# Eight sample rows in column groups, small tiles for the widest recurrence levels, and two reordered casts in a two-layer decoder step

## What is computed

```python
x = x + 0.5 * gate0 * swiglu_1(mod(rmsnorm(x)))
h = mod(rmsnorm(x))
(u_pool, hq, hf, hi, hg, aq, ak, av, iq, ik, iw, gl) = split(h @ w_in)
ya = pool_mix(u_pool) 
yb = rmsnorm(hgrn_scan(hq, f(hf), 1 - f(hf), hi)) * silu(hg)
yc = sparse_attention(aq, ak, av, iq, ik, iw)
x = x + gate1 * (sum(sigmoid(gl_b) * (y_b @ w_b)) @ w_out)
x = x + 0.5 * gate2 * swiglu_2(mod(rmsnorm(x)))
```

## Time and profile before

| | us |
|---|---|
| median of three runs | 2718.54 |
| the three runs | 2718.4, 2721.93, 2718.54 |
| the profiled execution, its own time | 2719.41 |
| its span in the trace | 2717.3 |

### The profile page before, as it was taken

The page is one execution under the profiler, slowest core; times in us unless marked ns, Lnnn a source line. Parts: engine busy times, 40 slices in busy tenths (PEclk is TensorE's granted clock), DMA queues, the critical chain, the costliest instruction groups (busy, mean ns, idle before and its releaser), DMA issues. The chain is left out here.

```text
span 2717.3 us, 53697 instructions
## 1 busy us (share of the span) xinstructions
PE 2652.4 (98%) x22268; PEld 2517.3 (93%) x22268; DVE 922.8 (34%) x2323; ACT 831.4 (31%) x1313; POOL 1103.5 (41%) x886
## 2 busy tenths in 40 slices
PE   6999999999999999999999999999999999999998
PEld 4999998999888989999989999989998889899998
DVE  4111113266794441111131111134677824311111
ACT  2321222222465233212233212232234632332221
POOL 4434345333223354344553444542333225444443
PEclk9999999999999999999999999999999999999999
DMA  6334345312223343332533322641122134222222
GB/s 246 139 125 148 136 162 178 115 47 83 76 71 97 125 144 136 124 107 92 185 128 138 121 97 93 201 154 63 63 77 83 57 106 173 73 91 85 94 90 80
DMA packets 107055, 312.88 MB, mean 115 GB/s; under 512 B 18476, under 2 KB 45130, under 8 KB 89434
## 3 DMA queue, kind: packets, MB, share of 16 engines
q1 hardware_dynamic: 97952, 290.60, 31.8%
q10 hardware_dynamic: 8906, 19.44, 2.0%
HBM read 299.56 MB, written 10.66 MB: 114 GB/s over the span
## 5 line engine op out<-in xcount | busy, mean ns | idle before, releaser
L948 POOL TENSOR_TENSOR w_lo<-raw,w_hi 128x512 fp32r<-128x512 f32 (+1 forms) x800 | 1011.3, 1295 | 1579.2 <-ACT w_hi L1022 1531.6
L2163 PE MATMUL bank<-h_hi,w_hi 128*128 128x260 f32 x3744 | 1067.7, 285 | 2.9 <-ACT silu_g L1069 2.4
L2164 PE MATMUL bank<-h_hi,w_lo 128*128 128x260 f32 x3744 | 1053.9, 281 | 0.0
L2165 PE MATMUL bank<-h_lo,w_hi 128*128 128x260 f32 x3744 | 1053.7, 281 | 0.0
L2163 PEld LDWEIGHTS bank<-h_hi,w_hi 128*128 128x128 f32 x3744 | 703.6, 188 | 38.0 <-issue 35.9
L2164 PEld LDWEIGHTS bank<-h_hi,w_lo 128*128 128x128 f32 x3744 | 703.9, 188 | 0.0
L2165 PEld LDWEIGHTS bank<-h_lo,w_hi 128*128 128x128 f32 x3744 | 703.6, 188 | 0.0
L1022 ACT CAST w_hi<-raw 128x2048 fp32r<-128x2048 f32 (+3 forms) x219 | 376.4, 1719 | 481.1 <-PE bank L2165 376.9
L2163 PE MATMUL bank<-mid_hi,w_hi 128*128 128x260 f32 x1232 | 351.1, 285 | 0.0
L2165 PE MATMUL bank<-mid_lo,w_hi 128*128 128x260 f32 x1232 | 348.5, 283 | 0.0
L2164 PE MATMUL bank<-mid_hi,w_lo 128*128 128x260 f32 x1232 | 348.3, 283 | 0.0
(11 more groups left out here) (334 smaller groups left out, 3315.7 us busy)
## 6 DMA issues: line engine op xcount, KB each, us to landing
raw<-in_w SPq DMA_DIRECT2D x120, 1024.0 KB, 4.9
raw<-in_w SPq DMA_DIRECT2D x64, 512.0 KB, 4.4
raw<-in_w SPq DMA_DIRECT2D x32, 768.0 KB, 4.3
ada_ring<-in_ada SPq DMA_DIRECT2D x82, 256.0 KB, 5.3
raw<-in_w SPq DMA_DIRECT2D x32, 640.0 KB, 4.1
ada_ring<-in_ada SPq DMA_DIRECT2D x57, 320.0 KB, 5.3
ada_ring<-in_ada SPq DMA_DIRECT2D x57, 192.0 KB, 5.3
ada_low<-in_ada SPq DMA_DIRECT2D x20, 256.0 KB, 5.2
```

The source lines that it names most:

```text
L948: last = pool.tensor_tensor(w_lo[j][:, cols], raw[j][:, cols], w_hi[j][:, cols].bitcast(F32), ALU.subtract)
L2163: mm(out, wh(wb), xh(xb), start=(n == 0), stop=False)
L2164: mm(out, wl(wb), xh(xb), start=False, stop=False)
L2165: last = mm(out, wh(wb), xl(xb), start=False, stop=(n == len(blocks) - 1))
```

## The change

1. The padded sample group is gone. `sample_rows` multiplies the eight columns of `h_s` (stationary, 128 x 8) by the raw fp32 weights, in four matmuls of 64 weight columns per `k`, each into its own 32 rows of a PSUM bank (column tiles, as in the conditioning products). `sample_group` is all eight `k` of a name. u's and hi's rows run inside the `k` loop of `first_token`, aq0's ahead of its group 0, iq's, aq1's and kv's between kbT and delta, hg's at the last level of head 3. ACT copies the four pieces out, and clears three tiles a layer, whose padding was written with the group before.
2. Since TensorE now reads `raw`, SP's load of a slot also waits for the sample rows of the slot that lay there.
3. Level 32 is eight matmuls of 32 x 32, level 64 four of 64 x 64.
4. The filler moves up by one group, and head 0 has nothing between levels 32 and 64.
5. ACT copies kbT ahead of the cast.
6. POOL's held split no longer waits.

```diff
@@ SP @@
             def load_mix(l, slot):
                 j = slot % 2
                 sp.wait_ge(w_split[j], slot_use(l, "mix", slot // 2) + PRIMED)
+                if slot >= 2 and MIX[slot - 2] in TOKENS:
+                    wait_main(sp, mix_unit(l, MIX[slot - 2], 0))
...
             def load_gates(l, stage, slot, tiles):
+                if (stage, slot) == ("ga0", 1):
+                    wait_main(sp, mix_unit(l, "hg", 0))
@@ POOL @@
                         first = 0
-                        gap = N_SUB * l + {"up00": 0, "mix": 1, "up10": 2}.get(stage, 0)
-                        if gap > 0 and stage in ("up00", "mix", "up10"):
-                            split(l, stage, 0, 0)
-
-                            pool.wait_ge(h_lo_ready, 9 * gap + 2)
-                            split(l, stage, 0, 1)
-                            first = 1
                         with pool.Fori(first, slots // 2) as r:
@@ ACT @@
+                if u == 0:
+                    for a in range(4):
+                        src = bank[unit % 4][32 * a:32 * a + NB, 0:HD]
...
+                    last.then_inc(done, 1)
+                    return
...
-                if hf == 1:
-                    head_after(l, "mix", MIX.index(f"H{hd}"))
+                if hf == 1 and hd == 0:
+                    head_after(l, "mix", MIX.index("H0"))
...
+                zeros = h_hi[:, :, COLS:].bitcast(F32)
+                steps.note(s.copy(rot[:, TT].rearrange("p r n -> p (r n)").rearrange("p (k n) -> p k n", k=KT), zeros))
+                steps.note(s.copy(vals[:, TT].rearrange("p (k n) -> p k n", k=2), zeros[:, 0:2, 0:HD]))
+                steps.note(s.copy(h_g[:, TT].rearrange("p (k n) -> p k n", k=4), zeros[:, 0:4, 0:HD]))
...
                     turned_keys(l, hd)
+                    if hd + 1 < HH:
+                        head_after(l, "mix", MIX.index(f"H{hd + 1}"))
@@ PE @@
+            def sample_rows(l, name, k):
+                slot = MIX.index(name)
+                unit = mix_unit(l, name, 0)
+                if k == 0:
+                    pe.wait_ge(w_loaded[slot % 2], slot_loads(l, "mix", slot // 2))
+                    take_unit(unit)
+                for a in range(4):
+                    at = k * 256 + a * HD
+                    last = mm(bank[unit % 4][32 * a:32 * a + NB, 0:HD], h_s[:, k, :], raw[slot % 2][:, at:at + HD],
+                              start=(k == 0), stop=(k == KT - 1))
...
                 for k in range(KT):
                     wait_h(N_SUB * l + 1, k)
-                    for u in range(3 if k < KT - 1 else 2):
-                        token_tile(l, "u", u, 0, k)
...
+                    sample_rows(l, "u", k)
+                    for g in (0, 2):
+                        last = token_tile(l, "u", g, k)
+                    if k < KT - 1:
+                        sample_rows(l, "hi", k)
+                for g in (1, 3):
+                    for k in range(KT):
+                        last = token_tile(l, "u", g, k)
                     last.then_inc(main_full, 1)
+                sample_rows(l, "hi", KT - 1)
...
-                        if 1 <= n < 5 and hd + n > 1:
-                            token_group(l, BESIDE[hd], n)
-                        elif n >= 5 and hd + 1 < HH:
+                        if hd == 0 and n in (2, 3):
+                            token_group(l, BESIDE[0], n)
+                        elif hd == 0 and n in (4, 5, 6):
+                            hgrn_projection(l, 1, n - 4)
+                        elif hd > 0 and 1 <= n < 5:
+                            token_group(l, BESIDE[hd], n - 1)
+                        elif 0 < hd < HH - 1 and n >= 5:
                             hgrn_projection(l, hd + 1, n - 5)
...
+                            sample_group(l, "hg")
                             token_group(l, "hg", 0)
...
-                            last = mm(out[:, cs], hk[hd % 2][:, cs], qt[:, cs], start=True, stop=True)
+                            if n < MASKED:
+                                last = mm(out[:, cs], hk[hd % 2][:, cs], qt[:, cs], start=True, stop=True)
+                                continue
+                            for s0 in range(0, P, 2 * h):
+                                keys = slice(c * P + s0, c * P + s0 + h)
+                                rows = slice(c * P + s0 + h, c * P + s0 + 2 * h)
+                                last = mm(out[s0:s0 + h, rows], hk[hd % 2][:, keys], qt[:, rows], start=True, stop=True)
...
                     if hd + 1 < HH:
-                        token_group(l, BESIDE[hd + 1], 0)
+                        sample_group(l, BESIDE[hd + 1])
...
                 token_group(l, "hg", 3)
-                token_group(l, "hg", 4)
                 outputs(HH - 1)
```

More of the change, by code:

```diff
@@ L116 @@
 BESIDE = ("aq0", "iq", "aq1", "kv")
+TOKENS = ("u", "hi", "aq0", "iq", "aq1", "kv", "hg")
 MIX_SOURCE = {n: SLOT0["token"] + i for i, n in enumerate(("u", "hi", "hg", "aq0", "aq1", "kv", "iq", "thin"))}
@@ L1137, in token_unit @@
                 wait_main(act, unit)
-                tl = slice(2 * u, 2 * u + 2) if u < 2 else slice(TT, TT + 1)
-                nt = 2 if u < 2 else 1
-                src = bank[unit % 4][:, 0:256 * nt].rearrange("p (t n) -> p t n", t=nt)
                 done = main_taken[unit % 4]
+                if u == 0:
+                    for a in range(4):
+                        src = bank[unit % 4][32 * a:32 * a + NB, 0:HD]
+                        cols = slice(a * HD, (a + 1) * HD)
+                        if name == "u":
+                            last = s.copy(pool_u[0:NB, TT, cols], src)
+                        elif name == "hi":
+                            last = s.copy(h_i[0:NB, TT, cols], src)
+                        elif name == "hg":
+                            last = s.activation(h_g[0:NB, TT, cols], src, ACT.Silu)
+                        elif name == "kv" and a >= 2:
+                            last = s.copy(vals[0:NB, TT, (a - 2) * HD:(a - 1) * HD], src)
+                        else:
+                            last = s.copy(rot[0:NB, TT, (list(range(ROT))[heads_of[name]])[a], :], src)
+                    last.then_inc(done, 1)
+                    return
+                tl = slice(2 * u - 2, 2 * u)
+                src = bank[unit % 4][:, 0:512].rearrange("p (t n) -> p t n", t=2)
                 if name == "u":
@@ L2327, in wait_mix, with token_tile @@
                 return slot % 2
-            def token_tile(l, name, u, i, k):
+            def token_tile(l, name, g, k):
                 j = MIX.index(name) % 2
-                t = 2 * u + i
-                out = bank[mix_unit(l, name, u) % 4][:, 256 * i:256 * (i + 1)]
-                cols = slice(t * P, (t + 1) * P)
+                u, i = divmod(g, 2)
+                out = bank[mix_unit(l, name, u + 1) % 4][:, 256 * i:256 * (i + 1)]
+                cols = slice(g * P, (g + 1) * P)
                 wcols = slice(k * 256, (k + 1) * 256)
@@ L2345, in token_group, with sample_group @@
                 if i == 0:
-                    take_unit(mix_unit(l, name, u))
+                    take_unit(mix_unit(l, name, u + 1))
                 for k in range(KT):
-                    last = token_tile(l, name, u, i, k)
-                if i == 1 or u == 2:
+                    last = token_tile(l, name, g, k)
+                if i == 1:
                     last.then_inc(main_full, 1)
+            def sample_rows(l, name, k):
[8 more added lines that the diff above has]
+                              start=(k == 0), stop=(k == KT - 1))
+                if k == KT - 1:
+                    last.then_inc(main_full, 1)
+            def sample_group(l, name):
+                for k in range(KT):
+                    sample_rows(l, name, k)
             def first_token(l):
                 wait_mix(l, "u")
-                for u in range(3):
+                for u in (1, 2):
                     take_unit(mix_unit(l, "u", u))
@@ L2803, in _ @@
                         ada_turn(ADA_PARTS * (sub + 2))
-                        for g in range(5):
+                        for g in range(4):
                             token_group(l, "hi", g)
```

10 lines of the change are left out of this document (6 added, 4 removed).

## The result

| | kernel before | changed kernel |
|---|---|---|
| median of the first comparison, us | 2718.47 (4 runs) | 2690.05 (2687.39 to 2692.44, 4 runs) |
| ratio to before, 95% interval | | 0.9893 [0.9875, 0.991] |
| the same, timed again later | 2717.8 (7 runs) | 2689.98, ratio 0.9901 [0.9884, 0.9918] |
| span of the profiled execution | 2717.3 | 2688.8 |

The change takes 28.4 us off, 1.1%. The forecast was 2698 with a range down to 2691, so the direction was right and the gain was 8 us larger than forecast, just outside the range.

A forecast was written before the change was run, and what follows sets the result against it. TensorE's queue of matmuls, busy for 98% of the span, was taken as the bound. Terms of -9.75 us a layer, -19.5 in two, and -1.0 at the boundaries gave 2698 against 2718.54, range 2691 to 2712.

The forecast's parts named there:

- no rival: Whole kernel: record sets price, 2734 (0.08); floor at 28 ns, 2707 (0.2); late H0, 2712 (0.1); no change, near 2718 (0.04).
- H0 didn't come late: Rival at hi's end: H0's load, held behind u's sample rows, lands late; each layer loses 7.0 us, 2712; chance 0.1.
- the new waits in heads and tail: Outputs of three heads wait 0.2 us each, +0.6; VectorE late at the layer's tail, +0.4 a layer.
- the wide levels: Levels 32 and 64 in the heads shrink to 0.53 and 0.70 us: -1.0 a layer, ends -1.7 and +0.9.
- The record's price: Sample rows on TensorE: 17 ns for each 64-column record, 64 records a group.
- The switch: TensorE around each sample group: 0.26 us for going from whole-array matmuls to tiles and back.
- the five names: Sample groups of aq0, iq, aq1, kv and hg: each 2.90 us group becomes 1.35, -7.75 us a layer.
- hi: hi's projection: its sample rows move into the first-token loop, so its own stretch loses 2.90 us.
- first token: First-token stage with u's and hi's sample rows: VectorE sets the pace at 1.32 us a step, 17.3 against 17.51, -0.2.
- The filler of head 0: Head 0, nothing between levels 32 and 64: TensorE stands for VectorE's products, +1.1 us, ends 0.8 and 1.5.
- a sign of being wrong: Heads 1 to 3: new waits of TensorE for VectorE above 0.3 us would show the prediction wrong.
- The boundaries: Three later FFN boundaries with POOL's split released: -0.35 us each, between -1.0 and +0.8, -1.0 in all.

The follow-up runs named there:

- doubled groups: Changed kernel with the ten sample groups of aq0, iq, aq1, kv and hg each running their 64 records twice: 2696.25 us, ratio 0.9915.
- whole levels again: Changed kernel with levels 32 and 64 as four full matmuls again: 2694.91 us, ratio 0.9911.
- the cut filler: Changed kernel with head 0's 24 matmuls ahead of level 32 cut in two, half moved between levels 32 and 64: 2689.95 us, ratio 0.9902.
- the moved step: Changed kernel with VectorE's last rotary step of heads 1 and 2 issued after the products for level 64: 2687.81 us, ratio 0.9889.

## Why the prediction was right and wrong

The direction and the mechanism held: TensorE's queue got shorter, the sample groups were the main part of it, and no rival came true. H0 didn't come late: ACT's cast of it waited 0.35 us for the load, and TensorE reached H0's products at 487.86 without a wait:

```profile
476.25 1.91 ACT L1022 CAST w_hi<-raw 128x2048 fp32r<-128x2048 f32 x1 [0.35 <-DMA raw<-in_w]
...
487.86 0.36 PE L2185 MATMUL bank<-h_hi,w_hi 128*128 128x260 f32 x1
```

What failed are two steps of the sum: the new waits in heads and tail, put at +1.0 a layer where old waits went and the term came out near -1.4, and the wide levels, put at -1.0 where they gave -2.0. Its own range ended at 2692 because it let the waits fall to nothing at best, and not below. The sizes, term by term, for the mean of the two layers:

- **The record's price.** 17 ns was taken, 13.4 to 13.9 measured (doubled groups). The switch was taken as 0.26 us and is about 0.4 in the heads (4.14 - 2.48 is 1.66 us less than the 2.95 of a token group, so 1.29 for a sample group with both changeovers, less 64 x 0.0137), and less for aq0, whose group follows matmuls on half-array tiles (its stage grew by 1.0 in all). The two errors nearly cancel: a group costs 1.29 instead of 1.35. With 2.95 instead of 2.90 for a removed group among the heads' levels, the five names give about -8.6 instead of -7.75.
- **hi** -2.78 against -2.90, and **first token** -0.77 against -0.2. There the step of 1.25 us was right. That VectorE would set the pace at 1.32 was wrong for all but the last two steps: it was ahead by the time TensorE started, and the steps stand 1.25 apart. With the split held this stage took 27.60 and 27.96, 0.3 more than before, so the release makes the gain here and the rows cost 0.3.
- **The wide levels** -2.0 against -1.0 (whole levels again). This is the first mis-sized term, and it lies below the lower end of -1.7. Level 32 takes 0.37 and not 0.53, level 64 0.58 and not 0.70.
- **The filler of head 0.** +1.1 was taken. With whole levels, where the levels' own saving is out of it, head 0 holds 1.26 us of standing; in the changed kernel 0.96 ahead of level 64, of which the cut filler gets 0.8 back. Right in place and size.
- **The new waits in heads and tail.** +0.6 and +0.4 were taken, and this is the step that failed most. Neither came: the outputs wait 0.39 behind delta and level 0 as they waited 0.37 before, and the stretch from the end of the recurrence to the next norm takes 312.35 us in layer 0, where it took 312.39. A wait that it hadn't priced did come, the 0.51 ahead of level 64 in heads 1 and 2, above the 0.3 that the prediction named as a sign of being wrong. It is VectorE's rotary step, as the moved step shows, and is counted with the levels here, since with whole levels 0.18 of it is left. But older waits went. With whole levels, heads 1 and 2 are still 2.14 us shorter than before and head 3 2.16, where a sample group for a token group explains 1.66 to 1.7: some 0.45 to 0.5 a head more, -1.4 a layer where +1.0 was put.
- **The boundaries.** -1.0 was taken, +0.16 measured. The first of them landed beyond the upper end of 0.8, at 1.06, because of something that the prediction didn't have, a half-clock stretch behind the longer wait. The sum is in part luck of the two executions: the kernel before has a stretch at the boundary into layer 1's up10, too, and without any stretch the three would have come to about -0.5, -0.5 and -0.4.

What went in the heads can be placed. From the start of level 16 to kbT, head 1 takes 12.15 us before and 11.64 with whole levels, so all of its 0.5 lies around the levels 32 and 64. POOL's, VectorE's and TensorE's timelines in head 1 before, with VectorE's last operation ahead of the level's operands:

```profile
568.87 6.63 POOL L948 TENSOR_TENSOR w_lo<-raw,w_hi 128x512 fp32r<-128x512 f32 x4 [16.26 <-ACT w_hi L1022]
...
569.00 2.52 DVE L781 TENSOR_TENSOR rot<-rot,rope_q 128x1280 f32<-128x1280 f32 x1
...
574.51 1.13 PE L2482 MATMUL bank<-qm,hk 128*128 128x128 f32 x8 [0.43 <-DVE qm L1796]
```

and in head 1 of the changed kernel:

```profile
562.50 6.64 POOL L955 TENSOR_TENSOR w_lo<-raw,w_hi 128x512 fp32r<-128x512 f32 x4 [14.35 <-ACT w_hi L1022]
...
562.42 1.49 DVE L782 TENSOR_TENSOR rot<-rot,rope_q 128x1280 f32<-128x1280 f32 x1
```

Before, POOL's split began 0.13 us ahead of the rotary step, which took 2.52 us, and TensorE waited 0.43 ahead of level 32. Now it begins 0.08 behind it, the step takes 1.49, and level 32 at 567.43 has no wait. So it is in heads 1 and 2 of both layers in all 12 traces with the change, and the other way round in all four of these heads before. In head 3 a wait of 0.31 ahead of kbT went as well; hg's sample rows now stand ahead of level 64 there. That the order of arrival of the split and the rotary step is the cause was only read from these rows; no run moved the split alone, so it stays open how much of the 1.4 us it explains.

The sum by these terms: 4.6 us a layer more than predicted, 9.2 in two, less 1.2 at the boundaries: 8.0, the distance between 2698 and 2690.

## What to carry to other kernels

Few rows against many weights paid here as the stationary side of four column tiles: the price of a record went with its moving columns (55 ns for 256, 14 for 64), and one tile alone lost the whole gain. When TensorE's filler is shortened, look through every copy that stood hidden under it and put it ahead of whatever has time, here the cast; and price the waits of a rearranged stretch from both sides, since an old wait can go as easily as a new one can come. Where the times scatter by more than an edit is worth, compare fixed stages of the traces, which here repeated to 0.05 us as long as the clock stayed up.

## What the runs showed of the hardware that was not expected

- A small product of VectorE, 128x64, with both inputs in SBUF took 1.01 us beside POOL's split and some 0.23 without it, while the product just ahead of it, which reads a PSUM bank, took 0.21 beside the same split; a rotary step took 2.52 us when the split began 0.13 us ahead of it, and 1.49 when it began 0.08 us behind it.
- At the boundary into up10, TensorE stands 2.45 us in layer 0 and 2.88 in layer 1 with the held split, and 3.23 and 3.65 with the released one. A half-clock stretch followed the longer waits in 6 of 10 traces in layer 0 and in 9 of 10 in layer 1 (in 5 in both), and the shorter ones in 0 of 3 and 1 of 3 (the kernel before and two experiments). With the released split the stage takes 22.15 without a stretch and 23.70 with one of 3.4 us, so that costs 1.55 us. What else decides whether a stretch comes was not tried.
- 64 records of eight stationary and 64 moving columns take 0.89 us in four column tiles and 3.66 us in one.
